# One decoder layer on one core: two passes over the weights, or two fronts and three backs

## The reference

```
proj = x @ w_in                     # z, xBC, dt, uv, gates
y_a  = gated norm of SSD scan(conv(xBC), dt) * silu(z)   # 8 groups, chunks of 128 tokens, state carried
y_b  = gelu(u) * (tril(W_s) @ layer_norm(gelu(v)) + b)   # within a chunk
h    = layer_norm(ALPHA * x + (g_a * (y_a @ w_a) + g_b * (y_b @ w_b)) @ w_out)
q, s = h @ w_q, s = q . keys        # 8 heads, two halves, 128 keys each
expert ids, gates = softmax(top 16 of the 16 x 16 sums)  # 128 experts a token, out of 16384
y    = layer_norm(ALPHA * h + sum_k gate_k * gelu(h . u_tab[e_k]) * v_tab[e_k])
```

## Time and profile before

| | us |
|---|---|
| median of 3 runs | 5152.17 (5151.67 to 5163.72) |
| the profiled execution, its own time | 5156.45 |
| its span | 5154.2 |
| pass 0 (first tile product to the end) | 34.8 to 1830.7 |
| pass 1 | 1830.7 to 3780.0 |
| tail | 3780.0 to 5154.2 |
| mean granted TensorE clock | 0.955 of 2.4 GHz |
| DMA | 1674.51 MB, mean 325 GB/s |

### The profile page before, as it was taken

One profiled execution on the slowest core, in us unless ns is written; L12 is line 12 of the kernel. 1 busy time (PEld: TensorE's weight loads), 2 busy tenths in 40 slices (PEclk: granted clock), 3 DMA queues, 4 the chain that ended last, 5 costly groups with the idle time before them and its releaser, 6 DMA issues. The chain is left out here.

```text
span 5154.2 us, 48498 instructions
## 1 busy us (share of the span) xinstructions
PE 4519.3 (88%) x18494; PEld 3366.5 (65%) x18494; DVE 2798.2 (54%) x3713; ACT 859.0 (17%) x1941; POOL 2251.5 (44%) x1647
## 2 busy tenths in 40 slices
PE   8999999999999978888879899899867777887776
PEld 6878878888887867777768788787743332332222
DVE  3565622000001668888877865566876655464445
ACT  2333321100000123333311110000111111110000
POOL 3676830000000235555543733454588874364442
PEclk9999999999999989999989999999989999999999
DMA  6666664445555489999999999999999999999998
GB/s 201 212 219 218 200 192 137 136 148 165 166 154 162 123 328 393 416 418 408 416 376 418 416 416 416 384 417 418 375 420 421 421 422 419 401 412 421 421 422 369
DMA packets 331807, 1674.51 MB, mean 325 GB/s; under 512 B 47200, under 2 KB 62112, under 8 KB 195872
## 3 DMA queue, kind: packets, MB, share of 16 engines
q0 software_dynamic: 160640, 1133.71, 53.7%
q1 hardware_dynamic: 165768, 536.51, 30.2%
q10 hardware_dynamic: 5168, 1.19, 0.1%
HBM read 1633.31 MB, written 37.89 MB: 324 GB/s over the span
## 5 line engine op out<-in xcount | busy, mean ns | idle before, releaser
L596 PE MATMUL psum<-rows_a,w_ring 128*128 128x264 f32 x6656 | 1501.4, 387 | 13.2 <-PEq L551 8.8
L596 PEld LDWEIGHTS psum<-rows_a,w_ring 128*128 128x128 f32 x6656 | 1265.5, 191 | 234.0 <-issue 19.1
L596 PE MATMUL psum<-x_and_spare,w_ring 128*128 128x256 f32 x5632 | 1264.8, 385 | 59.2 <-PEq L551 21.4
L596 PEld LDWEIGHTS psum<-x_and_spare,w_ring 128*128 128x128 f32 x5632 | 1080.5, 193 | 230.1 <-issue 70.8
L404 POOL DMA_INDIRECT rows_a<-in_peer_u,expert x384 | 728.9, 1898 | 887.9 <-DVE rows_a L459 821.7
L459 DVE SCALAR_TENSOR_TENSOR rows_a<-rows_a,h_tokens 128x2048 f32<-128x2048 f32 x388 | 890.4, 2296 | 330.1 <-DMA rows_a<-in_peer_u,expert 307.6
L404 POOL DMA_INDIRECT rows_a<-in_peer_v,expert x382 | 514.3, 1346 | 366.6 <-PE psum L503 170.8
L503 PE MATMUL psum<-rows_b,diags 128*128 128x512 f32 x1008 | 477.0, 621 | 177.3 <-ACT diags L493 129.6
L503 PE MATMUL psum<-rows_a,diags 128*128 128x512 f32 x1008 | 488.7, 634 | 153.4 <-ACT diags L493 101.5
L503 PEld LDWEIGHTS psum<-rows_b,diags 128*128 128x128 f32 x1008 | 190.7, 197 | 461.7 <-issue 292.7
L503 PEld LDWEIGHTS psum<-rows_a,diags 128*128 128x128 f32 x1008 | 194.7, 201 | 446.4 <-issue 302.8
(11 more groups left out here) (375 smaller groups left out, 3391.1 us busy)
## 6 DMA issues: line engine op xcount, KB each, us to landing
w_ring<-in_w_tiles SPq DMA_DIRECT2D x896, 512.0 KB
rows_a<-in_state_ssm POOLq DMA_DIRECT2D x32, 512.0 KB, 6.3
out_ssm_sample<-rows_a POOLq DMA_DIRECT2D x32, 512.0 KB, 5.2
rows_a<-acum_rows_dram SPq DMA_DIRECT2D x16, 512.0 KB, 5.1
rows_a<-smp_bc_dram POOLq DMA_DIRECT2D x8, 1024.0 KB, 8.1
acts_by_token<-late SPq DMA_DIRECT2D x16, 512.0 KB, 6.6
branch_b<-acum_rows_dram SPq DMA_DIRECT2D x16, 512.0 KB
rows_a<-in_xT SPq DMA_DIRECT2D x3, 2048.0 KB, 14.0
```

Of the source, the lines that this page charges most:

```text
L596: last = pe.matmul(o, w[:, k * P:(k + 1) * P], x[:, k, :], start=start and k == 0, stop=stop and k == KB - 1)
```

## The change

The blocks no longer pass the stages in pairs. A `Front` is scan and gating, a `Back` the stages from the gates on. Front 0 has block 0 and the samples (n = 136), front 1 blocks 1 to 3 (n = 384). Back a has block 0 and the samples (136) and follows front 0; back b has block 1 (128) and back c blocks 2 and 3 (256), both after front 1. The weight tiles of the fronts are read twice, those of the backs three times. Block 0's 128 slots lie in front 1 and back b (11 in each scan group, 8, 10, then 22), block 1's in back c. Back a chooses two heads of block 0; the other six are chosen in front 1's scan groups 0 to 5, and block 1's late heads during back c's gates. The first expert buffers are four for u and three for v.

With it: for the samples GpSimd stops after the state is stored, and VectorE makes the product with C and the sum (`prod`, 1024 elements, per unit); there are five state buffers, and the B and C rows of a group are loaded when VectorE has summed the group before. Tiles of front 0, back a and back b are loaded whole, with one DMA. A third chunk in front 1 gets its own place in the order of TensorE, ScalarE and VectorE. In front 1 u is kept in a ring of eight tiles, the norm's squares in two quarters, and branch b is written over v once v has been stored. v's mean is summed on VectorE in both fronts, h's in backs a and b. Branch a's activations are read into tiles of their own, so that x is still there for the residual; only back c loads it again. Semaphores of later stages are cleared by GpSimd at the start of the stage after the next.

The diff, cut to what sets order and cost:

```diff
-N_GROUPS = N_TILES - FT
-
-
-PASS_CHUNKS = ((0, 2), (2, 2))
-PASSES = len(PASS_CHUNKS)
-RINGS = (3, 3)
-RING = max(RINGS)
-BLOCK_PASS = [i for i, (first, count) in enumerate(PASS_CHUNKS) for _ in range(count)]
+BACK_GROUPS = N_TILES - FT - O_GATE
+
+
+FRONT_CHUNKS = ((0, 1), (1, 3))
+BACK_CHUNKS = ((0, 1), (1, 1), (2, 2))
+BACKS_OF = ((0,), (1, 2))
+RING = 3
+STREAM, WHOLE = [], []
+for _f, _backs in enumerate(BACKS_OF):
+    STREAM += ORDER[:O_GATE]
+    WHOLE += [_f == 0] * O_GATE
+    for _b in _backs:
+        STREAM += ORDER[O_GATE:]
+        WHOLE += [_b < 2] * (N_TILES - O_GATE)
...
-STEPS_B = (13, 20, 16, 32, 15, 32, 16, 3, 18)
+STEPS_F = (11, 8, 10)
+STEPS_B = (6, 3, 5, 3, 1, 4)
+STEPS_C = (35, 18, 36, 17, 3, 19)
...
-    BUFS = 3
+    BUFS = 5
...
+            pool.wait_ge(self.summed, r - self.BUFS + 1)
...
+        if GT * g > self.first:
+            pool.wait_ge(self.summed, GT * g - self.first)
...
+        pool.sem_inc(self.ready, 1)
         pool.dma_start(self.target[v], s).then_inc(self.state_out[r % self.BUFS], 16)
-        x = self.xb
-        o(pool.tensor_tensor(x[:], s, self.bc[:, 1], ALU.mult))
-        o(pool.tensor_tensor(x[:, :, 0:64], x[:, :, 0:64], x[:, :, 64:128], ALU.add))
-        o(pool.tensor_tensor(x[:, :, 0:32], x[:, :, 0:32], x[:, :, 32:64], ALU.add))
-        if r >= 2 * GT:
-            pool.wait_ge(self.summed, r // GT - 1)
-        o(pool.tensor_tensor(self.fold[:, r // GT % 2, t], x[:, :, 0:16], x[:, :, 16:32], ALU.add))
-        pool.sem_inc(self.ready, 1)
         self.last = r
-    def sums(self, dve, g):
-
-        r = g - self.first // GT
-        dve.wait_ge(self.ready, GT * (r + 1))
-        dve.tensor_reduce(self.y[:, g], self.fold[:, r % 2], AX_X, ALU.add).then_inc(self.summed, 1)
+    def sums(self, dve, o, v):
+
+        g, t, r = v // GT, v % GT, v - self.first
+        dve.wait_ge(self.ready, r + 1)
+        o(dve.tensor_tensor(self.prod[:], self.state[:, r % self.BUFS], self.bc[:, 1], ALU.mult))
+        o(dve.tensor_reduce(self.y[:, g, t], self.prod[:], AX_X, ALU.add))
+        dve.sem_inc(self.summed, 1)
...
     def load_weight(self, sp, p):
-        while self.loaded < PASSES * N_TILES and self.loaded - RINGS[self.loaded // N_TILES] <= p:
+        while self.loaded < len(STREAM) and self.loaded - RING <= p:
             q = self.loaded
-            for half, used in enumerate((self.half_used, self.w_used)):
-                w = slice(half * WCOLS // 2, (half + 1) * WCOLS // 2)
-                if self.w_held[q] >= 0:
-                    sp.wait_ge(used, self.w_held[q] + 1)
-                sp.dma_start(self.w_slots[self.w_slot[q]][:, w],
-                             self.a["w_tiles"][ORDER[q % N_TILES]][:, w]).then_inc(self.w_in[self.w_slot[q]][half], 16)
+            slot, tile = self.w_slots[q % RING], self.a["w_tiles"][STREAM[q]]
+            if WHOLE[q]:
+                if q >= RING:
+                    sp.wait_ge(self.w_used, q - RING + 1)
+                sp.dma_start(slot, tile).then_inc(self.w_in[q % RING][0], 16)
+            else:
+                for half, used in enumerate((self.half_used, self.w_used)):
+                    w = slice(half * WCOLS // 2, (half + 1) * WCOLS // 2)
+                    if q >= RING:
+                        sp.wait_ge(used, q - RING + 1)
+                    sp.dma_start(slot[:, w], tile[:, w]).then_inc(self.w_in[q % RING][half], 16)
             self.loaded += 1
...
-        for i, (scan, v, u, gate, wb, wa, mix, ln, q) in ((1, STEPS_B),):
-            for g in range(G):
-                put(i, [("ssd", g, c) for c in range(9)], scan)
-            put(i, tiles("v", FT), v)
-            put(i, tiles("u", FT), u)
-            put(i, tiles("gate", 2 * FT), gate)
-            put(i, tiles("wb", FT), wb)
-            put(i, tiles("wa", FT), wa)
-            put(i, tiles("out", FT), mix)
-            put(i, tiles("ln", 2), ln)
-            put(i, tiles("q", FT), q)
+
+        def back(name, gate, wb, wa, mix, ln, q):
+            put(name, tiles("gate", 2 * FT), gate)
+            put(name, tiles("wb", FT), wb)
+            put(name, tiles("wa", FT), wa)
+            put(name, tiles("out", FT), mix)
+            put(name, tiles("ln", 2), ln)
+            put(name, tiles("q", FT, 6 if q < 10 else 0), q)
+
+        scan, v, u = STEPS_F
+        for g in range(G):
+            put("f1", [("ssd", g, c) for c in range(9)], scan)
+        put("f1", tiles("v", FT), v)
+        put("f1", tiles("u", FT), u)
+        back("b", *STEPS_B)
+        back("c", *STEPS_C)
...
-            ex = Experts(self, 4, 8, LAG)
+            ex = Experts(self, 4, 3, 8, LAG)
...
+            self.stage(lambda st: self.ssd(st, ps, xs, spare, room, m_acts, None), None)
+            self.stage(lambda st: self.sgu(st, ps, xs, self.region(spare)(KB, ps.n), yb, yb, FT, m_acts, None, None), None)
+            self.stage(lambda st: self.back(st, one, xs, branch, xs, yb, room, m_acts, spare, kept, None, h_smp, None), None)
...
+            self.stage(lambda st: self.ssd(st, ps, xs, spare, room, late, ex), ex)
+            self.stage(lambda st: self.sgu(st, ps, xs, yb, u_ring, yb, FT // 2, late, small, ex), ex)
+            self.stage(lambda st: self.back(st, one, head(xs), branch, head(xs), head(yb), self.htok[:, 2, :], late,
+                                            self.htok[:, 2, :], self.kept_one, yb[:, 0:2, 0:one.n], None, ex), ex)
+            self.stage(lambda st: self.back(st, two, rest(xs), [rest(xs), rest(yb)], rest(xs), rest(yb), room, late,
+                                            flat(self.htok[:, CH - 2:CH, :]), last, None, None, ex), ex)
...
+        heads = [(0, p) for p in range(EARLY, PH)] if ex else []
+        choose_at = {(i, 2): i for i in range(len(heads))}
+        share_at = {(i, 6): i for i in range(len(heads))}
...
                     project(g, CT + 2)
-                    if nc_ > 1:
+                    if wide:
                         chunk_b(g, 0)
                         chunk_a(g, 1)
                     project(g, CT + 3)
-                    if nc_ == 1:
+                    if not wide:
                         chunk_b(g, 0)
                     if g < G - 1:
                         project(g + 1, 0)
-                    if nc_ > 1:
+                    if wide:
                         chunk_b(g, 1)
+                        chunk_a(g, 2)
+                        if g < G - 1:
+                            project(g + 1, 1)
+                        chunk_b(g, 2)
...
                     spread_chunk(g, 0)
+                    sums(g, 3)
                     expert(g, 5)
                     weigh(g, 0)
-                    if nc_ > 1:
-                        dve.wait_ge(b_done, nc_ * g + 1)
-                        next_state(g, 0)
-                        outputs(g, 0).then_inc(y_done, 1)
-                        dve.wait_ge(y_done, nc_ * g + 1)
+                    if wide:
+                        chunk(g, 0)
+                        spread_chunk(g, 1)
                     expert(g, 6)
-                    if nc_ > 1:
-                        spread_chunk(g, 1)
+                    if wide:
+                        weigh(g, 1)
+                        if g < G - 1:
+                            conv(g + 1, 0)
+                        chunk(g, 1)
+                        spread_chunk(g, 2)
                     expert(g, 7)
-                    if nc_ > 1:
-                        weigh(g, 1)
-                    if nc_ > 1 and g < G - 1:
-                        conv(g + 1, 0)
-                    dve.wait_ge(b_done, nc_ * g + nc_)
-                    outputs(g, nc_ - 1)
-                    next_state(g, nc_ - 1).then_inc(y_done, 1)
-                    dve.wait_ge(y_done, nc_ * g + nc_)
+                    if wide:
+                        weigh(g, 2)
+                        if g < G - 1:
+                            conv(g + 1, 1)
+                    chunk(g, nc_ - 1)
...
+                    if m == 0 and ps.last:
+                        dve.wait_ge(self.v_out, 16 * (ps.i + 1))
+                    dve.tensor_tensor(yb[:, m, 0:np_], ut[:, m % ring, 0:np_], mix, ALU.mult)
+                    if smp and m in range(4, 8):
+                        smp.sums(dve, o, GT * (G - 1) + m - 4)
...
+        late = [(1, p) for p in range(EARLY, PH)] if ps.last else []
+        late_at = {2 + 5 * i: i for i in range(len(late))}
+        late_share = {c + 3: i for c, i in late_at.items()}
...
-                load_ya(xs, 1)
+                load_ya(ya_high, 1)
                 for p in range(ps.pos + P_WB, ps.pos + P_WA):
                     self.load_weight(sp, p )
-                load_ya(yb, 0)
+                sp.wait_ge(self.v_out, 16 * (ps.front + 1))
+                load_ya(ya_low, 0)
                 for p in range(ps.pos + P_WA, ps.pos + P_OUT):
                     self.load_weight(sp, p )
                 if ps.last:
```

(8 more changed lines are left out.)

646 lines of the change are left out of this document (371 added, 275 removed).

## The result

The changed kernel takes 5363.6 us, the median of four runs from 5356.7 to 5366.3, against 5153.6 beside it: 1.040 times as long, 95% interval 1.0383 to 1.0419. The forecast was 5223 with a range up to 5330, so the time lies 34 us outside it. The profiled execution has a span of 5361.2 us, 207.0 more than that of before and 136 more than the sum.

A forecast was written before the change was run, and what follows sets the result against it. TensorE-bound with idle DMA, then both near limits, then a DMA-bound tail. Parts 1071 + 1388 + 442 + 950 and tail 1374 gave a 5225 us span, 5223 on the median's footing; own range 5170 to 5260, wider 5115 to 5330.

The forecast's parts named there:

- Part 1: Block 0 and samples through all stages up to q (136 columns): 1071 us with the 35 us start, its scan 430.
- part 3: Later stages of block 1 (128 columns) with 22 expert slots: 442 us, bounds 425 and 490.
- Part 4: Later stages of blocks 2 and 3 (256 columns) with 128 slots: DMA-bound, 950 us, bounds 935 and 975.
- Part 2: Shared scan and gating of blocks 1 to 3 (384 columns) with 106 slots: 1388 us, groups 120.5 each.
- 17 for tiles that come late: In part 3, 17 us allowed for late weight tiles, as DMA's 409 us nearly fills the stage with three ring slots.
- at the 406 to 413 GB/s that these stages show: In part 4, 393 MB moved at the rate of the old later stages: 950 us.
- the tail: Last stretch of the kernel, DMA-bound at 413 GB/s with the same 264 slots: unchanged at 1374 us.
- the term for held products: In part 1's scan, GpSimd could hold each of four new VectorE products by 1.9 us, 7.6 us a group.
- VectorE off the path in both scans: Rival for the scans of parts 1 and 2: groups at 43.5 and 116.5, 100 us less, 5123 us; chance 0.19.
- VectorE setting the second scan at 128 a group: Rival for part 2's scan: 60 us more, 5285; or part 1's groups at 60 us, 5287; chance 0.18.
- The weight load that doesn't hide behind 128 columns: Rival for narrow tiles: exposed weight loads make a tile 6.1 us, the kernel some 5950 us; chance 0.04.
- the ratio used ahead: Skill's 81 ns sustained against 56 isolated, 1.45: narrow tiles 5.3 us, kernel some 5700; the forecast set it aside.

The follow-up runs named there:

- part 3 with 4 slots: Changed kernel with 18 of part 3's 22 expert slots moved ahead to v and u of part 2: 5313.5 us, 1.0300 of before.
- the runs with six and nine slots: Changed kernel, six slots per part 2 scan group instead of eleven, 40 to part 3: 5445.7 us; nine, with 24 and 28 in v and u plus the combined repairs: 5274.7.

## Why the prediction was right, and where it was wrong

**Where the change's time goes.** The 222.6 us of the later stages are four sums. Part 1's later stages (305.1 + 164.2) and part 3 with 4 slots (434.1) take 903.4 where one stretch took 861.2, 42 more. Ends and norm waits are little of it: TensorE's idle time is 40 us against 31, while its tile products alone are busy for 845.5 us against 803.5. A tile of 136 columns and one of 128 take 3.75 + 3.56 us where one of 264 took 7.1, some 21 us over 112 tiles; the rest of the 42 wasn't taken apart. The gathers beside narrow tiles are 72 (65 by the mean). Part 4 carries 386 MB where the old stretch carried 360 (406 GB/s by 886.1 us), 26 MB at 406 GB/s: 65. The six choices in it are 41, or 33 by the whole of part 4. Together 212 to 220. What the change wins, 30 us in the scans, is small because TensorE was nearly full in the first and the idle DMA was never what bound it; this was the forecast's reason, and it stood.

**Right.** The direction and its reason. The price of narrow tiles: 3.75 and 3.56 us against 3.7 and 3.55. Part 1's gates and branches 305 against 297, u 76.8 against 82, output and q 164.2 against 165. Part 2 within 8 us: its groups 110 to 129, 120.1 on average against 120.5, 3 us of it VectorE, as the runs with six and nine slots show; the last 158.3 against 168. Part 4's branches, output and q by DMA's pace.

**Wrong: "17 for tiles that come late" in part 3.** The step put DMA (409 us) and TensorE (398) side by side and took their overlap as nearly free. Measured 506.3. The gathers cost 65 to 72 on a stage of 434. Two rates that each fit don't fit together when a burst of 2.1 MB takes most of the pipe for some microseconds and the consumer has two tiles in hand. The bound of 490 was too low as well.

**Wrong: part 4 "at the 406 to 413 GB/s that these stages show".** Pass two's later stages had no head of another block to choose; the change puts six into the first of them. I had the choice's price on VectorE (6.6 us) and charged it to the scan, where it costs less, and not here, where it costs 6.8 each: 41 of the 44 us in the gates, 33 by the whole of part 4. The 950 itself was partly luck: it divides 393 MB by 413 GB/s, which is the tail's rate; at the 406 of the stages before it would have been 968, but only 386 MB were moved, 951 us at 406.

**Mis-sized: part 1's scan, 430 against 442.** The groups are 52 to 58 us where I had 52, the last 65 to which 14 were allowed. The sums' products were never held: 1220 ns for all 28, not 3.1 us. The convolution form was, 771 ns on average where 0.69 us was allowed. VectorE's groups by form of after, and a row each of VectorE's and GpSimd's timelines:

```profile
L1389 DVE SCALAR_TENSOR_TENSOR conv_acc_f<-raw_f,g_par,conv_acc_f 128x128 f32<-128x128 f32 x144 | 111.1, 771 | 31.7 <-ACT conv_acc_f L1249 23.3 <-DVE smp_y L340 4.5
L339 DVE TENSOR_TENSOR rows_a<-rows_a,h_tokens 128x1024 f32<-128x1024 f32 x28 | 34.2, 1220 | 0.5
L340 DVE TENSOR_REDUCE smp_y<-rows_a 128x8 f32<-128x1024 f32 x28 | 34.2, 1220 | 1.0
...
222.22 1.22 DVE L339 TENSOR_TENSOR rows_a<-rows_a,h_tokens 128x1024 f32<-128x1024 f32 x1
...
222.31 2.88 POOL L327 TENSOR_TENSOR rows_a<-rows_a,dt_smp 128x1024 f32<-128x1024 f32 x1
```

VectorE is busy for 38 us a group, not 49, and the group takes 54: what sets it is the order of short waits between VectorE, ScalarE and TensorE, which the sum had at 3 us. Two errors of opposite sign, so that the total of this stage is nearer than its terms. By the Trainium skill ("SBUF — State Buffer", the section on the two separate sides) whichever of a VectorE operation with two SBUF inputs and a GpSimd one starts first holds the shared ports to its end. This trace agrees, and shows why the term for held products failed. All 36 convolution records longer than 0.8 us started while a GpSimd operation ran, and ended about 0.15 us behind it. No product of the sums started while one of GpSimd's large operations ran. Six times GpSimd's multiplication of the state (L327) started 0.1 us behind a product, as above, and then it took 2.87 us on average where the others take about 1.9; its mean is 2115 ns where it was 1925. It was the products' place in the order that spared them.

**Mis-sized: v of part 1, 62 against 72.6.** 2 MB of weights of the gating stand ahead of the fifth tile in SP's queue; TensorE waits 6.9 us for tiles there. With wide tiles that was covered.

**The tail,** 1384 against 1374, isn't explained: DMA moves 411 GB/s against 413, and the runs' tails lie between 1379 and 1388.

**The rivals.** VectorE off the path in both scans: no. The runs give its price, 47.5 us in the first (what the sums cost; GpSimd's loop remains) and 28 in the second, 76 together, where the rival had 100; the rival's end of 5123 was not to be had even so, since parts 3 and 4 ate more. VectorE setting the second scan at 128 a group: only in three groups of the first seven, 123.0, 128.6 and 123.3. The weight load that doesn't hide behind 128 columns: no, by the windows above. The Trainium skill ("TensorE: Matmul & The Clock Gate", "Back-to-back issue gap") would have put a narrow tile at 5.3 us by the ratio used ahead; the measured 3.75 decides against it, and the weight loads, busy 300 of 305 us in part 1's gates and branches, just hide.

## What to carry to other kernels

Splitting a stage into narrower ones to let transfers start earlier costs little in products (here 0.2 us for two narrow tiles against a wide one) and a good deal in slack: the time of a tile halves, the time to load it doesn't, and a ring that was deep becomes shallow. Before adding gathers to such a stage, compare the burst, not the mean: what lands in the time of the tiles in hand if the other queue takes most of DMA for that long. And where DMA is full, price every operation that stops the engine which frees the buffers, here a choice of 6.7 us on VectorE, at its whole length; in the gates, moving the wait that the profile named gave 3 us, leaving out the choices 41.
